# The element order of the gate copy: contiguous read and stepped write in place of stepped read and short-run write

## The chip, the cores and the metric

The kernel runs on one core of one Trainium2 chip. The time is device microseconds of that core for one execution. Five engines take part: TensorE (PE in the profile, its weight loads PEld), VectorE (DVE), ScalarE (ACT), GpSimd (POOL) and SyncE (SP), which here only issues DMA transfers.

## The reference

One layer of a streaming encoder for 512 tokens of width 1024: a token-mixing half (windowed attention beside a gated position mixer), and then a PEER channel mixer. The change lies in the channel mixer. It picks, for each token and each of 8 heads, 16 experts out of 16384 and sums them with softmax weights:

```
q = (xt @ w_query).reshape(T, PEER_HEADS, 2, D_HALF)
s = jnp.einsum('thpd,hpnd->thpn', q, sub_keys)
top_s, top_i = lax.top_k(s, PEER_TOPK)
...
ids = i1 * N_KEYS + i2                 # expert = key 1 * 128 + key 2
gates = softmax(best_s)
a = jnp.einsum('tkd,td->tk', expert_down[idb], xb)
act = gelu(a) * gb
y = jnp.einsum('tk,tkd->td', act, expert_up[idb])
```

## The kernel before, in words

The first stages (up to about 446 us of the trace) make the token-mixing half and the scores, and pick 128 experts for each token. Of the 512 tokens, 128 are done by gathering their experts' rows. For the other 384 all 16384 experts are multiplied densely, in 128 tiles of 128 experts; the tile's result is multiplied by a gate that is zero where the token did not pick the expert.

These dense gates are made in the **gate stage**, which is where the change lies. For each token, a 128 x 128 matrix (key 2 on the partitions, key 1 along the row) is the product of two small matrices that hold one row for each of the token's 128 picks: `onehot2` (a 1 at the pick's key 2) and `gated1` (the gate at the pick's key 1). The work goes in 48 turns of 8 tokens, with two sets of buffers used in turn (u = 0, 1). In each turn:

- DVE writes six of the eight onehot2 matrices in one instruction (line 1117) and six of the eight gated1 matrices in six instructions (line 1121).
- POOL writes the other two gated1 matrices (line 525), after it has copied their scalars (line 522).
- ACT writes the other two onehot2 matrices (lines 757 and 761).
- PE multiplies (line 1463): two groups (s = 0, 1) of four tokens, each group into one PSUM bank. The group s = 0 waits for DVE alone, the group s = 1 for POOL and ACT too. Before it overwrites a bank it waits for the copy of two turns ago.
- ACT copies each bank (128 partitions x 512 elements: four tokens t with 128 keys i each) into `stage` (line 766), an SBUF tile that holds 128 keys x 128 tokens in each partition, so that the tokens of one key lie side by side and one key is 512 bytes from the next.

ACT's program runs in this order: the two copies of turn m, then its part of the one-hot rows of turn m + 2. The stage tiles are two; every 16 turns (one block of 128 tokens) SyncE writes a full one to device memory (lines 406 and 426): the first two blocks while the gate stage runs, the third in four pieces after it. The tiles' gates are read back from there in the last stage.

The last stage (from 574 us to the end) is a loop over the 128 tiles of experts: down product (lines 1482 to 1484), Gelu (line 793), times the gate (line 1166), up product (lines 1493 to 1495). Its first down weights are in SBUF while the gate stage still runs; ACT rounds them (line 787) right after its last gate copy.

Of the kernel before, what the change touches and what calls it, by code (L numbers as in the profile page):

```python
# [66 lines left out]
TB = 8  # L67
# [58 lines left out]
def build_block(nc, x, c, w_ada, b_ada, g_pre_mix, g_post_mix, g_pre_ffn, g_post_ffn, w_in, attn_sinks,  # L126
                sgu_norm, sgu_w, sgu_b, w_out, peer_query, peer_keys, peer_down, peer_up, down_t, out):
    ctx = ExitStack()
    with ctx:
# [109 lines left out]
        stage = [r(f"stage{i}", [KEYS, P]) for i in range(2)]  # L239
# [29 lines left out]
        bank = [ctx.enter_context(nc.psum_tensor(f"bank{i}", [P, 512], F32)) for i in range(8)]  # L269
# [305 lines left out]
        def _(act):  # L575
# [187 lines left out]
            def gates_out(b, i, u):  # L763
                for s in range(2):
                    act.wait_ge(pe_g, b * 32 + 4 * i + 2 * u + s + 1)
                    act.activation(
                        stage[b % 2][:, :, bass.ds(i * (2 * TB) + u * TB + 4 * s, 4)],
                        bank[1 + 2 * u + s][:].rearrange("p (t i) -> p i t", t=4),
                        ACT.Copy).then_inc(act_g, 1)

            for u in range(2):
# [2 lines left out]
            for b in range(GB):  # L774
                if b >= 2:
                    act.wait_ge(stored[b % 2], 16)
                with act.Fori(0, turns - 1 if b == GB - 1 else turns) as i:
                    for u in range(2):
                        gates_out(b, i, u)
                        hot_rows(b * 2 * turns + 2 * i + u + 2, u)  # L780
            for u in range(2):
                gates_out(GB - 1, turns - 1, u)
# [749 lines left out]
```

## Time and profile before

| | |
|---|---|
| time, median of 3 runs | 1676.28 us (1675.06 to 1676.77) |
| profiled execution, its own time | 1676.28 us |
| its span | 1674.2 us |
| mean granted TensorE clock | 0.964 |
| PE busy | 1509.4 us (90%) |
| DVE busy | 1192.8 us (71%) |
| ACT busy | 632.3 us (38%) |
| POOL busy | 711.3 us (42%) |

Busy shares are means over stages that are limited by different engines, so the stage around the change has to be read by itself. The gate copies run from 453.65 to 573.97 us of the span. The granted clock is a share of the full 2.4 GHz.

### The profile page before, as it was taken

The page shows a single profiled execution, that of the slowest core. Times are in us where ns is not written, and L with a number is a line of the kernel's source. Part 1 is how long each engine was busy: PE and PEld are TensorE (multiplying, and loading weights), DVE is VectorE, ACT ScalarE, POOL GpSimd, SP SyncE. Part 2 cuts the span into 40 slices and gives each one's busy share as a digit, 9 for nine tenths or more (in the row PEclk, how much of TensorE's full clock was granted, in tenths as well). Part 3 has the DMA queues.
Part 4 walks back from the last instruction along what each step waited for, and adds up shares of the span by engine and source line. Part 5 has one row for each costly group of instructions (what it writes and reads, how often), then busy time and mean ns, then how long its engine had stood idle before and what let it go on. Part 6 is the DMA issues. An engine that isn't in the chain of part 4 may idle for free.

```text
span 1674.2 us, 25887 instructions
## 1 busy us (share of the span) xinstructions
PE 1509.4 (90%) x7686; PEld 1291.7 (77%) x7686; DVE 1192.8 (71%) x2424; ACT 632.3 (38%) x1018; POOL 711.3 (42%) x715
## 2 busy tenths in 40 slices
PE   4999989676288779999999999999999999999995
PEld 3475537554277769999999999999999999999994
DVE  6545437999799748777777777777777777777776
ACT  1114324333488623333333333333333333333332
POOL 0000003555599627544444444444444444444441
PEclk9999999887599989999999999999999999999998
DMA  9942201110017899877777777877777778777762
GB/s 325 372 176 101 76 25 38 50 50 13 0 53 212 250 344 362 302 274 276 273 275 275 281 273 277 277 279 276 278 276 276 278 276 277 279 276 276 278 242 100
DMA packets 186503, 372.34 MB, mean 222 GB/s; under 512 B 19753, under 2 KB 103281, under 8 KB 186481
## 3 DMA queue, kind: packets, MB, share of 16 engines
q1 hardware_dynamic: 149088, 237.57, 42.5%
q0 software_dynamic: 36864, 134.23, 22.0%
q10 hardware_dynamic: 528, 0.26, 0.1%
q8 instruction: 11, 0.18, 0.0%
q14 instruction: 12, 0.09, 0.0%
HBM read 344.76 MB, written 27.26 MB: 222 GB/s over the span
## 4 chain that ended last, share of the span: by engine, by line
PE 63%; DVE 12%; issue 4%; DVEq 2%; SPq 1%; DMA 1%; ACT 1%; POOL 0%; POOLq 0%; ACTq 0%
PE bank L1482 10%; PE bank L1484 10%; PE bank L1483 10%; PE bank L1494 10%; PE bank L1495 10%; PE bank L1493 10%; DVE gated L1121 4%; DVE topi L1030 1%; DVEq L1121 1%; SPq L406 1%; DVE top L1027 1%; DVE cand L1052 1%; DVE pick L1045 1%; DVE score L1034 1%; DVE onehot L1117 1%
## 5 line engine op out<-in xcount | busy, mean ns | idle before, releaser
L1482 PE MATMUL bank<-h2hi,dhi 128*128 128x384 f32 x1024 | 345.4, 337 | 14.6 <-DVE dlo L1135 14.6
L1484 PE MATMUL bank<-h2hi,dlo 128*128 128x384 f32 x1024 | 345.2, 337 | 0.0
L1483 PE MATMUL bank<-h2lo,dhi 128*128 128x384 f32 x1024 | 344.5, 336 | 0.0
L1495 PE MATMUL bank<-uhi,alo 128*128 128x512 f32 x768 | 301.3, 392 | 0.0
L1494 PE MATMUL bank<-ulo,ahi 128*128 128x512 f32 x768 | 301.0, 392 | 0.0
L1493 PE MATMUL bank<-uhi,ahi 128*128 128x512 f32 x768 | 298.6, 389 | 0.0
L543 POOL COPY idx_u<-ids 128x1 uint32 (+1 forms) x128 | 112.7, 881 | 343.6 <-DVE y L1156 343.5
L1166 DVE TENSOR_TENSOR acts<-gel,gate 128x384 f32<-128x384 f32 x128 | 71.5, 559 | 257.1 <-ACT gel L793 234.0
L545 POOL DMA_INDIRECT rows_u<-in_peer_up,idx_u x128 | 199.9, 1562 | 99.0 <-POOL idx_u L543 99.0
L1482 PEld LDWEIGHTS bank<-h2hi,dhi 128*128 128x128 f32 x1024 | 193.6, 189 | 20.4 <-DVE dlo L1135 10.1
L1483 PEld LDWEIGHTS bank<-h2lo,dhi 128*128 128x128 f32 x1024 | 193.4, 189 | 4.8
L1484 PEld LDWEIGHTS bank<-h2hi,dlo 128*128 128x128 f32 x1024 | 193.3, 189 | 0.0
L802 ACT ACTIVATE ahi<-acts 128x384 fp32r<-128x384 f32 x128 | 67.1, 524 | 329.1 <-PE bank L1495 321.6
L793 ACT ACTIVATE gel<-bank 128x384 f32<-128x384 f32 x128 | 62.9, 492 | 338.9 <-PE bank L1484 338.9
L1135 DVE TENSOR_TENSOR dlo<-down,dhi 128x1024 fp32r<-128x1024 f32 x128 | 156.7, 1225 | 45.4 <-ACT dhi L787 45.4
L545 POOL DMA_INDIRECT rows_d<-in_peer_down,idx_d x128 | 130.6, 1020 | 104.3 <-POOL idx_d L543 97.6
L1156 DVE SCALAR_TENSOR_TENSOR y<-rows_u,coef,y 128x1024 f32<-128x1024 f32 x128 | 164.0, 1281 | 5.2 <-DVE coef L1150 5.0
L1495 PEld LDWEIGHTS bank<-uhi,alo 128*128 128x128 f32 x768 | 144.1, 188 | 30.3
L1144 DVE SCALAR_TENSOR_TENSOR junk<-rows_d,h2nat 128x1024 f32<-128x1024 f32 x128 | 157.0, 1227 | 14.6 <-DVE y L1156 7.5
L1494 PEld LDWEIGHTS bank<-ulo,ahi 128*128 128x128 f32 x768 | 144.1, 188 | 27.7
L1493 PEld LDWEIGHTS bank<-uhi,ahi 128*128 128x128 f32 x768 | 144.3, 188 | 27.2
L1177 DVE TENSOR_TENSOR ulo<-up,uhi 128x1024 fp32r<-128x1024 f32 x128 | 156.6, 1224 | 0.9 <-ACT uhi L804 0.8
(202 smaller groups left out, 2224.1 us busy)
## 6 DMA issues: line engine op xcount, KB each, us to landing
down<-in_down_t SPq DMA_DIRECT2D x128, 512.0 KB, 4.4
up<-in_peer_up SPq DMA_DIRECT2D x128, 512.0 KB, 3.4
ada<-in_w_ada SPq DMA_DIRECT2D x12, 2048.0 KB, 16.2
gate<-gates_dram SPq DMA_DIRECT2D x128, 192.0 KB, 4.0
gates_dram<-stage SPq DMA_DIRECT2D x2, 8192.0 KB, 30.4
wq<-in_peer_query SPq DMA_DIRECT2D x16, 512.0 KB, 4.0
gates_dram<-stage SPq DMA_DIRECT2D x4, 2048.0 KB, 14.3
w_in_sb<-in_w_in SPq DMA_DIRECT2D x2, 2048.0 KB, 20.0
```

Of the source, the lines that this page charges most:

```text
L543: ch.link(gp.tensor_copy(idx[k][:], ids[:, bass.ds(n, 1)]))
L545: return gp.indirect_dma_start(rows_[k][:], None, table[0], bass.IndirectOffsetOnAxis(ap=idx[k][:, 0:1], axis=0))
L1135: ve.tensor_tensor(dlo[s][:], down[s][:], dhi[s][:].bitcast(F32), ALU.subtract).then_inc(dve_dlo, 1)
L1144: ve.scalar_tensor_tensor(out=junk[:], in0=rows_d[k][:], scalar=1.0, in1=h2nat[:], op0=ALU.mult, op1=ALU.mult, accum_out=dots[:, k:k + 1]) ...
L1156: ve.scalar_tensor_tensor(out=y[:], in0=rows_u[k][:], scalar=coef[:, k:k + 1], in1=y[:], op0=ALU.mult, op1=ALU.add).then_inc(dve_add, 1)
L1177: ve.tensor_tensor(ulo[s][:], up[s][:], uhi[s][:].bitcast(F32), ALU.subtract).then_inc(dve_ulo, 1)
L1482: pe.matmul(bank[s][:, 0:TD], dhi[s][:, k, :], h2hi[:, k, 0:TD], start=k == 0, stop=False)
L1483: pe.matmul(bank[s][:, 0:TD], dhi[s][:, k, :], h2lo[:, k, 0:TD], start=False, stop=False)
L1484: last = pe.matmul(bank[s][:, 0:TD], dlo[s][:, k, :], h2hi[:, k, 0:TD], start=False, stop=k == KT - 1)
L1493: pe.matmul(got[:], ahi[s][:, tokens], uhi[s][:, half], start=first, stop=False)
L1494: pe.matmul(got[:], ahi[s][:, tokens], ulo[s][:, half], start=False, stop=False)
L1495: done = pe.matmul(got[:], alo[s][:, tokens], uhi[s][:, half], start=False, stop=last)
```

## The change

One instruction of the gate stage, the copy from a PSUM bank to `stage`, goes over the same 512 elements of each partition in another order. Before, key is the outer and token the inner dimension; after, token is the outer and key the inner.

```
                     act.activation(
-                        stage[b % 2][:, :, bass.ds(i * (2 * TB) + u * TB + 4 * s, 4)],
-                        bank[1 + 2 * u + s][:].rearrange("p (t i) -> p i t", t=4),
+                        stage[b % 2][:, :, bass.ds(i * (2 * TB) + u * TB + 4 * s, 4)].rearrange("p i t -> p t i"),
+                        bank[1 + 2 * u + s][:].rearrange("p (t i) -> p t i", t=4),
                         ACT.Copy).then_inc(act_g, 1)
```

| | PSUM read | SBUF write |
|---|---|---|
| before | each element 128 words (512 bytes) from the one before, every fourth time back | runs of 4 adjacent words (16 bytes), then 512 bytes on |
| after | 512 adjacent words | each element 512 bytes from the one before, 128 times, then back and one word on |

The same values land at the same addresses. No instruction is added, removed or moved on any engine, and every wait and every signal stays; the copy occurs 96 times (48 turns x 2 banks).

## Rows read from the trace of the kernel before

**Rows 1.** The page, part 1: busy time of each engine over the span.
```profile
PE 1509.4 (90%) x7686; PEld 1291.7 (77%) x7686; DVE 1192.8 (71%) x2424; ACT 632.3 (38%) x1018; POOL 711.3 (42%) x715
```

**Rows 2.** Chain of work that ended last, 560 to 640 us: start, length, what.
```profile
564.92 1.00 DVE gated L1121 x4
566.93 1.50 DVE gated L1121 x6
...
571.29 2.06 PE bank L1463 x16
573.37 0.61 ACT stage L766
574.07 8.69 DMA gates_dram<-stage
```

**Rows 3.** Busy time in two stretches; PEclk is the granted clock.
```profile
core 0: us, PE busy (x) PEld busy (x) DVE busy (x) ACT busy (x) POOL busy (x), PEclk, DMA share, GB/s
480.00:520.00 40.00, 32.53 (x256) 29.56 (x256) 40.00 (x113) 34.86 (x81) 37.19 (x49) 1.00 0.65 184
520.00:560.00 40.00, 32.51 (x256) 29.55 (x256) 40.00 (x113) 34.87 (x80) 37.19 (x49) 1.00 0.74 208
```

**Rows 4.** Timeline of one turn: start, length, instruction, in brackets the idle before it.
```profile
565.92 0.60 ACT L766 ACTIVATE stage<-bank 128x512 f32 x1 [0.29 <-PE bank L1463]
566.26 2.05 PE L1463 MATMUL bank<-gated,onehot 128*128 128x128 f32 x16 [0.47 <-DVE gated L1121]
566.41 0.68 ACT L757 ACTIVATE onehot<-iota,pickT 128x128 f32<-128x128 f32 x2
566.92 1.72 DVE L1121 TENSOR_SCALAR gated<-iota,pickT 128x128 f32<-128x128 f32 x6
567.13 0.51 ACT L761 ACTIVATE onehot<-onehot,ones 128x256 f32<-128x256 f32 x1
567.55 0.60 ACT L766 ACTIVATE stage<-bank 128x512 f32 x1
568.44 0.60 ACT L766 ACTIVATE stage<-bank 128x512 f32 x1 [0.29 <-PE bank L1463]
568.57 0.94 DVE L1117 TENSOR_TENSOR onehot<-iota,pickT 128x768 f32<-128x768 f32 x1
```

**Rows 5.** Who waited for whom, 460 to 560 us: total, times, longest.
```profile
PE bank L1463 <- DVE gated L1121: 18.7, 40, 0.5
ACT stage L766 <- PE bank L1463: 11.8, 41, 0.3
```

**Rows 6.** Waits of the SP queue, 440 to 640 us.
```profile
SPq L410 <- DMA gates_dram<-stage: 30.0, 1, 30.0
SPq L426 <- ACT stage L766: 8.0, 1, 8.0
```

**Rows 7.** Groups of ACT instructions over the span: busy us, mean ns, idle before.
```profile
L679 ACT ACTIVATE wqhi<-wq 128x1024 fp32r<-128x1024 f32 x16 | 16.7, 1047 | 0.0
L793 ACT ACTIVATE gel<-bank 128x384 f32<-128x384 f32 x128 | 62.9, 492 | 338.9 <-PE bank L1484 338.9
L766 ACT ACTIVATE stage<-bank 128x512 f32 x92 | 54.8, 597 | 16.5 <-PE bank L1463 16.5
L718 ACT ACTIVATE score<-bank 128x512 f32<-128x512 f32 x16 | 8.9, 596 | 1.4 <-PE bank L1434 1.3
L624 ACT ACTIVATE kT<-bank 128x512 f32<-128x512 f32 x1 | 0.6, 597 | 7.2 <-PE bank L1328 7.2
```

**Rows 8.** Timeline of ACT at the start of the gate copies.
```profile
455.35 0.60 ACT L766 ACTIVATE stage<-bank 128x512 f32 x1 [1.11 <-PE bank L1463]
455.85 0.68 ACT L757 ACTIVATE onehot<-iota,pickT 128x128 f32<-128x128 f32 x2
456.56 0.51 ACT L761 ACTIVATE onehot<-onehot,ones 128x256 f32<-128x256 f32 x1
456.98 1.06 ACT L766 ACTIVATE stage<-bank 128x512 f32 x2
457.93 0.69 ACT L757 ACTIVATE onehot<-iota,pickT 128x128 f32<-128x128 f32 x2
```

**Rows 9.** A group of POOL instructions over the span.
```profile
L499 POOL TENSOR_TENSOR hit<-hit,topf 128x1024 f32<-128x1024 f32 x16 | 37.6, 2369 | 1.1 <-ACT hit L728 1.1
```

**Rows 10.** Timeline of PE, 380 to 386 us.
```profile
380.06 0.76 PE L1393 MATMUL bank<-h2hi,wqhi 128*128 128x512 f32 x1 [6.38 <-POOL wqlo L483]
...
382.33 0.63 PE L1395 MATMUL bank<-h2hi,wqlo 128*128 128x512 f32 x1
...
385.34 0.40 PE L1393 MATMUL bank<-h2hi,wqhi 128*128 128x512 f32 x1
```

**Rows 11.** Busy time and granted clock of two stretches there.
```profile
376.00:384.00 8.00, 3.94 (x10) 3.15 (x11) 7.97 (x52) 5.48 (x6) 8.00 (x4) 0.57 0.23 66
384.00:392.00 8.00, 8.00 (x44) 6.83 (x43) 7.90 (x36) 2.53 (x4) 3.06 (x2) 1.00 0.00 0
```

**Rows 12.** Timeline of ACT at the end of the gate copies.
```profile
572.48 0.60 ACT L766 ACTIVATE stage<-bank 128x512 f32<-128x512 f32 x1 [1.02 <-PE bank L1463]
573.37 0.60 ACT L766 ACTIVATE stage<-bank 128x512 f32<-128x512 f32 x1 [0.29 <-PE bank L1463]
573.87 1.99 ACT L787 ACTIVATE dhi<-down 128x1024 fp32r<-128x1024 f32 x2
```

## The prediction

> **What bounds the kernel now.** I start with the busy shares of the whole span: PE leads with 90%, ACT stands at 38% [rows 1]. That would say that nothing done to ACT matters. But a share over the span is a mean over stages, so I go to the stage that holds the copy. The chain of waits near its end reads, turn after turn, "DVE gated", and only at the very end PE, one copy of ACT, and then the store [rows 2]. The stretches of 40 us inside the stage say the same: DVE is busy for 40.00 of 40.00 us, ACT for 34.9, POOL for 37.2, PE for 32.5 at a granted clock of 1.00 [rows 3]. So DVE sets the pace of the gate stage, and ACT, at 87%, is not far behind. The whole question is how far.
>
> The timeline of one turn answers it [rows 4]. The second copies of two turns in a row start at 565.92 and 568.44, so a turn takes about 2.51 us (2.52 between rounded numbers; 48 turns are 120.5 us, and the copies run for 120.3 us). In each turn ACT waits for PE once, 0.29 us before the second copy (11.8 us in 41 waits between 460 and 560 us [rows 5]). That is less than ACT's true slack, because the first copy also starts before PE has finished the second bank. The true need of ACT is the time from start to start when it waits for nothing:
>
> - second copy to the first one-hot instruction: 566.41 - 565.92 = 0.49 us [rows 4];
> - the one-hot instructions up to the next copy: 567.55 - 566.41 = 1.14 us [rows 4];
> - the first copy when the second follows with no wait: 457.93 - 456.98 = 0.95 us for the two, less 0.49 for the second, is 0.46 us [rows 8].
>
> The sum is 2.09 us a turn against DVE's 2.51. The slack is 0.42 us a turn, 0.21 us for each of the two copies.
>
> **The change part by part.** It removes, adds and moves no instruction. It has two parts, both inside the copy.
>
> The read becomes contiguous. Today each element lies 512 bytes from the last, and the copy takes 597 ns. Copies of the same size that read PSUM in one run take 596 ns (scores) and 597 ns (keys) [rows 7]. So the stepped read costs nothing today, and the contiguous one gains nothing: 0. Even a faster copy would gain nothing, since ACT is not the bound of the stage; what a faster copy could save is its own 0.1 us once, at the end.
>
> The Trainium skill ("SBUF — State Buffer", Specifications) says that PSUM has 8-byte lines, SBUF 16-byte ones, and that an access which crosses to a new line every time pays. The 597 ns of the present copy, which hops lines on every read, does not bear this out for ACT's reads from PSUM. Its half on PSUM would give the contiguous read a gain, and the trace gives none; its half on SBUF would charge the new write, which puts one word in a line in place of four, but it has no figure.
>
> The write becomes stepped. Today it writes four adjacent words and then hops 512 bytes; after the change every word is a hop. No row of the trace has an ACT write of single words, so its price has to be bounded.
>
> - Lower end: a hop costs nothing, as it does on the read side and as the present hop after every fourth word does (597 ns against 596 [rows 7]). The copy stays at 0.60 us.
> - Upper end: nothing but a slower engine's pace is at hand. POOL takes 2369 ns for 1024 elements, 2.31 ns each [rows 9]. ACT's own element costs (597 - 492) / 128 = 0.82 ns, from its copies of 512 and 384 elements out of PSUM, with 597 - 512 x 0.82 = 177 ns fixed [rows 7]. At POOL's pace the copy would take 177 + 512 x 2.31 = 1360 ns, 0.76 us more.
> - The value that I take: each word needs one more step of ACT, so 512 elements cost what 1024 do. By the slope that is 597 + 512 x 0.82 = 1017 ns; the row of a 1024-element instruction reads 1047 ns [rows 7]. I take 1.03 us, 0.43 us more. It lies between the two ends and it is the nearest ACT row that takes more steps. I choose it above the lower end because the two hops are not alike: the free one in today's write comes once in four words, the new one comes with each word, so that there is nothing for it to hide behind.
>
> The Trainium skill has a measurement of the same kind, on another engine ("Vector Engine (DVE) Microarchitecture Reference", Measured stream behaviour on trn2): a VectorE op whose destination hops on every element takes 1.71 ns a column in place of 1.05, runs of two or more words are free, and one that steps by 24 words takes 2.50 ns. No run here shows it. With 1.71 ns the copy would be an estimated 177 + 512 x 1.71 = 1.05 us, and the end 22 us later.
>
> Now the sum. With 0.43 us more for each copy ACT needs 2.09 + 0.86 = 2.95 us a turn, more than DVE's 2.51, and it becomes the bound. Does anything else stop it at that pace? The order on ACT is copies of turn m, one-hot rows of turn m + 2. PE's group for turn m + 1 needs the one-hot rows that ACT finished before the copies of turn m, and PE needs 2.05 us for both groups [rows 4], less than 2.95. DVE may start turn m + 2 when PE is done with turn m, and it needs 2.51. So PE and DVE wait, and ACT does not.
>
> I place it in time from the rows. The second copy of turn 0 starts at 455.35 [rows 8], since it waits for PE and not for ACT. The copies of turn 1 then start at 455.35 + 0.49 + 0.43 + 1.14 = 457.41. Turns 1 to 45 have copies and one-hot rows: 45 x 2.95 = 132.75, so the copies of turn 46 start at 590.16. The last two turns have four copies and no one-hot rows: three at 0.46 + 0.43 and the last for its full 1.03, 3.70 us, and the end is at 593.86. Today it is at 573.37 + 0.60 = 573.97 [rows 12]. The gate stage becomes 19.9 us longer.
>
> **What hides it? Nothing.** After its last copy ACT goes on with rounding the down weights at 573.87 [rows 12], for which PE waits, and the store of the third block starts at 574.07, the next piece of the chain [rows 2]. SyncE had waited 30.0 us for the second block's store and then still 8.0 us for ACT's last copy [rows 6]. So neither the store nor the early loads are late; with a slower gate stage they are only earlier in comparison. From there all is as today, 19.9 us later. The profiled execution took 1676.28 us for a span of 1674.2, so 2.1 us lie around the span, and it is also the median of the runs. Forecast: 1676.3 + 19.9 = 1696 us, 1.2% slower. For copies between 1.01 and 1.07 us the same sum gives 1694 to 1700.
>
> **The rivals.**
>
> *A. The hop is free, or smaller than the slack: not slower.* ACT's writes leave at one word a step wherever they go, as its reads come in. The point from which it decides is 0.21 us a copy, that is 0.81 us: below that DVE keeps the pace of 2.51 us. For it: the read side and the present 16-byte runs at 597 ns. Against it: no row shows single-word writes. Time: 1676 us, at most 0.4 us more for the last two copies. Any gain would have to come out of a DVE that is never idle, and the copy does not touch it.
>
> *B. The hop costs more than a step.* Price by POOL's pace: a copy of 1.36 us, a turn of 2.09 + 1.52 = 3.61 us. The same placing gives 457.74 + 45 x 3.61 + 3 x 1.22 + 1.36 = 625.2, 51 us later: 1727 us. For it: the new step is the same power of two each time, so that successive words may meet in the same part of the memory. Against it: today's reads use the same step at full rate. The skill's 2.50 ns for a step of 24 words (same page and section) would be an estimated 1.46 us a copy and about 60 us.
>
> *C. PE loses its clock.* PE would work 2.05 of 2.95 us, 69% in place of 82%. In an earlier stage, after an idle time of 6.38 us, matmuls that take 0.40 us at the full level took 0.63 [rows 10], and the granted clock of that stretch was 0.57, against 1.00 in the next [rows 11]. If the gate stage fell to the lower level of 1.2 GHz, 2.05 us of PE would become about 4 and PE would be the bound: 1.5 x 47 = 70 us more, 1746 us. Against it: the idle times would be under 1 us each.
>
> **How the numbers follow.** Chances: forecast 0.75; A 0.12; B 0.09; C 0.02; and 0.02 for a gain that I cannot place, such as a better meeting of DVE and PE. What a measurement of this kernel can tell from no change is about 0.2%, 3.4 us. The forecast, B and C are slower by more, which is 0.86; A is the case of no change, 0.12, and the last case is faster, 0.02. The range has to hold 0.8: the forecast's own range is 1692 to 1704 (copies of 0.99 to 1.11 us by the same sum), and A is reached at 1676. I take 1675 to 1710, which leaves out B and C.
>
> **What the profile after would show.** The mean of the copy at line 766 near 1030 ns in place of 597, with every other ACT group as before. In the middle of the gate stage a turn of 2.95 us, ACT busy the whole time, DVE at 2.51 / 2.95, 85%, waiting for PE, and PE waiting for ACT's one-hot rows in its second group. The copies end near 594 us; from there the trace is today's, shifted. The granted clock stays at 1.00. If the copy reads 597 ns or anything up to 810, rival A holds and the turn stays at 2.51 us. If it reads well over 1.1 us, it is B; if the matmuls of line 1463 lengthen instead, C. My prediction is wrong in its mechanism if the copy lengthens by 0.43 us and the turn does not reach 2.9, since then ACT has slack that I did not see.

## The result, and the profile after

The changed kernel takes 1691.51 us (median of 4 runs, 1690.55 to 1692.72) against 1676.35 us (4 runs, 1675.06 to 1676.77) for the kernel before. The ratio is 1.0092, with a 95% interval of 1.0075 to 1.0109. It is 15.2 us slower. Forecast were 1696 us and 19.9 us more, with 1675 to 1710 as the range; the range of the forecast's own case, 1692 to 1704, was missed by half a microsecond.

The copy itself, among the groups of ACT instructions over the span (against [rows 7]):

```profile
L766 ACT ACTIVATE stage<-bank 128x512 f32 x92 | 89.3, 1072 | 3.1 <-PE bank L1463 3.1
L793 ACT ACTIVATE gel<-bank 128x384 f32<-128x384 f32 x128 | 62.9, 492 | 344.2 <-PE bank L1484 344.2
L757 ACT ACTIVATE onehot<-iota,pickT 128x128 f32<-128x128 f32 x96 | 31.5, 378 | 0.0
```

It went from 597 to 1072 ns, and its idle time before it from 16.5 to 3.1 us: ACT no longer waits for PE. The other ACT groups have the length they had, but for the first one-hot instruction (line 757), whose mean went from 391 to 378 ns. The two stretches in the middle of the stage (against [rows 3]):

```profile
480.00:520.00 40.00, 32.43 (x226) 27.10 (x224) 36.85 (x101) 39.54 (x72) 36.56 (x44) 1.00 0.51 144
520.00:560.00 40.00, 32.42 (x225) 27.23 (x226) 36.86 (x100) 39.55 (x71) 36.74 (x43) 1.00 0.60 171
```

DVE fell from 40.00 to 36.86 us, ACT rose from 34.87 to 39.55, and the granted clock stayed at 1.00. The stage has changed hands. In the same time PE did 225 matmuls in place of 256 and the turn is that much longer. PE's busy time hardly fell, since the 16 matmuls of a turn are counted as busy for about 2.4 us in place of 2.05; the count is the better reading. DMA traffic does not matter to the copy: its mean is 1075 ns from 460 to 490 us, where the DMA share is 0.00, and 1071 ns from 500 to 530 us, where it is 0.99. Who waited for whom, 460 to 560 us (against [rows 5]):

```profile
PE bank L1463 <- ACT onehot L761: 13.6, 31, 0.5
DVE onehot L1117 <- PE bank L1463: 6.7, 30, 0.2
PE bank L1463 <- DVE gated L1121: 2.1, 5, 0.5
```

The line "ACT stage waits for PE" is gone, PE waits for ACT's one-hot rows, and DVE, which had no wait in this stretch before, waits for PE. One turn in the timeline (against [rows 4]):

```profile
542.57 1.92 ACT L766 ACTIVATE stage<-bank 128x512 f32 x2
542.57 1.70 POOL L525 TENSOR_SCALAR gated<-iota,own 128x128 f32<-128x128 f32 x2 [0.17 <-POOL own L522]
542.90 2.38 PE L1463 MATMUL bank<-gated,onehot 128*128 128x128 f32 x16 [0.44 <-ACT onehot L761]
544.23 0.96 DVE L1117 TENSOR_TENSOR onehot<-iota,pickT 128x768 f32<-128x768 f32 x1 [0.23 <-PE bank L1463]
544.28 0.65 ACT L757 ACTIVATE onehot<-iota,pickT 128x128 f32<-128x128 f32 x2
544.97 0.51 ACT L761 ACTIVATE onehot<-onehot,ones 128x256 f32<-128x256 f32 x1
545.38 1.93 ACT L766 ACTIVATE stage<-bank 128x512 f32 x2
```

ACT has no gap, and no wait hides under the overlapping copies: PE ended its last matmuls at 545.28, before the two copies start at 545.38. The two copies take 544.28 - 542.57 = 1.71 us from start to start, the one-hot rows 1.10, the turn 2.81. Over the whole stage it is 2.83 us, from the starts of turn 1 and of turn 46, the last four copies:

```profile
457.51 1.94 ACT L766 ACTIVATE stage<-bank 128x512 f32 x2
...
585.03 3.59 ACT L766 ACTIVATE stage<-bank 128x512 f32<-128x512 f32 x4
588.43 1.99 ACT L787 ACTIVATE dhi<-down 128x1024 fp32r<-128x1024 f32 x2
```

(585.03 - 457.51) / 45 = 2.834 us. The last copy ends at 588.62 in place of 573.97, 14.65 us later, and the same store follows it in the chain of waits (against [rows 2]):

```profile
583.04 1.08 ACT stage L766
584.12 0.47 ACT onehot L757 x2
585.03 3.60 ACT stage L766 x4
588.72 8.69 DMA gates_dram<-stage
```

Behind the store the chain has the same links, down to the transfer of down weights for which ACT and then PE wait, first before and then after the change:

```profile
607.21 5.51 DMA down<-in_down_t
```

```profile
621.87 6.30 DMA down<-in_down_t
```

It ends at 612.72 before and at 628.17 after, 15.45 us later. So the gate stage gives 14.65 us and these transfers 0.8. The two profiled executions lie 1692.26 - 1676.28 = 16.0 us apart, the medians 15.2; what is left is no more than single executions differ by.

### The profile page after: what moved, and what is told of

The parts are those of the page before. It is cut to its first block, busy times and chain, and to the rows that moved or that the text cites. A ratio compares the mean times of both kernels' runs of the same rounds, so it can differ in the third digit from the quotient of the medians.

```text
span 1690.5 us, 25887 instructions
## 1 busy us (share of the span) xinstructions
PE 1524.0 (90%) x7686; PEld 1298.7 (77%) x7686; DVE 1196.7 (71%) x2424; ACT 661.7 (39%) x1018; POOL 721.4 (43%) x715
## 4 chain that ended last, share of the span: by engine, by line
PE 65%; DVE 8%; issue 4%; ACT 4%; SPq 1%; DMA 1%; POOL 0%; ACTq 0%; DVEq 0%; POOLq 0%
PE bank L1482 10%; PE bank L1484 10%; PE bank L1483 10%; PE bank L1494 10%; PE bank L1495 10%; PE bank L1493 10%; PE bank L1463 3%; ACT stage L766 2%; DVE topi L1030 1%; SPq L406 1%; DVE top L1027 1%; DVE cand L1052 1%; DVE pick L1045 1%; DVE score L1034 1%; ACT onehot L757 1%
```

## The experiments

A step is ACT's time for one element of a row, 0.82 ns in the prediction. Theory S: a word written by ACT that is not next to the word written before it takes two steps of ACT; the order of the read does not matter; and what the copy adds counts from the point where ACT needs more than DVE. Rivals: the read order or the shape of the loop costs (R), each new run costs whatever its length (L), only full 16-byte runs are fast (Q), the distance of the hop matters (B, N), or the turn is set by handovers and not by ACT. Each ratio is to the kernel before, run on the same chip. A line with + shows what the run's kernel has; `...` and `<...>` stand for parts left out.

**Write in one run** (e1)

```
-  stage[b % 2][:, :, bass.ds(i * 16 + u * 8 + 4 * s, 4)].rearrange("p i t -> p t i")
+  stage[b % 2][:].rearrange("p i t -> p (i t)")[:, bass.ds(i * 2048 + u * 1024 + s * 512, 512)]
```

> The copy reads its PSUM bank in one run, as in the changed kernel, and writes it to 512 adjacent words of stage (the gates land in other places, so the output is not the reference's). Theory S, a written word that is not next to the word before it takes two steps of ACT and the read order costs nothing: the copy is back at 597 ns, the turn at 2.51 us, the time at 1676 us. Rival R, the cost lies in reading the bank in token-outer order or in anything else of the new loop but the write: the copy stays near 1072 ns and the time near 1691 us.

Measured: 1675.54 us, ratio 0.9994 (0.9984 to 1.0004), copies of 598 ns, in the groups of ACT between 460 and 560 us, as for the next ones:

```profile
L766 ACT ACTIVATE stage<-bank 128x512 f32 x80 | 47.8, 598 | 11.6 <-PE bank L1463 11.6
```

All of the loss is gone with the read left contiguous. It was the write.

**Hop on both sides** (e4)

```
+  stage[b % 2][:].rearrange("p i t -> p (i t)")[:, <the same 512 words>].rearrange("p (t i) -> p i t", t=4)
+  bank[1 + 2 * u + s][:].rearrange("p (t i) -> p i t", t=4)
```

> The copy both reads and writes with a step of 128 words on every element (key outer, token inner on both sides; the gates land in other places, so the output is not the reference's). Theory S: the write hop costs as in the changed kernel and the read hop adds nothing: 1072 ns, 1691 us. Rival: the two costs add, or the read hop was hidden only because the write had runs: over 1300 ns, over 1710 us. Rival R: with the old read order the copy is back at 597 ns, 1676 us.

Measured: 1692.32 us, ratio 1.0092 (1.0075 to 1.0109), copies of 1085 ns:

```profile
L766 ACT ACTIVATE stage<-bank 128x512 f32 x71 | 69.7, 1085 | 0.0
```

The read hop adds 13 ns to 1072 even when the write hops too. With e1 this settles R: the read order costs next to nothing in either company.

**Runs of two words** (e3)

```
+  stage[...].rearrange("p i (h t) -> p h i t", h=2)
+  bank[1 + 2 * u + s][:].rearrange("p (h t i) -> p h i t", h=2, t=2)
```

> The copy writes runs of two adjacent words (8 bytes) and then hops 512 bytes; it reads two keys' tokens in step. Theory S in its form by pairs: two adjacent words are enough, 597 ns and 1676 us. Rival L, each new run costs something whatever its length: today's 128 runs are hidden but 256 would cost half of what 512 do, about 830 ns, a turn of 2.56 us, 1678 us. Rival Q, only a full run of four words goes at full rate: 1072 ns and 1691 us.

Measured: 1675.77 us, ratio 0.9995 (0.9986 to 1.0005), copies of 619 ns:

```profile
L766 ACT ACTIVATE stage<-bank 128x512 f32 x80 | 49.5, 619 | 10.6 <-PE bank L1463 10.6
```

Twice as many hops as before cost 22 ns, where L said about 230. L and Q fall. Two adjacent words are enough, where they begin on an even word, as they do here.

**A short step** (e5)

```
+  stage[b % 2][:].rearrange("p i t -> p (i t)")[:, <the same 512 words>].rearrange("p (i t) -> p t i", t=4)
```

> As the changed kernel (token outer, key inner, contiguous read), but the 128 words of a token are written 4 words (16 bytes) apart in place of 128 words, into a window of 512 adjacent words (the gates land in other places, so the output is not the reference's). Theory S, a word not next to the last costs one more step whatever the distance: 1072 ns, a turn of 2.83 us, 1691 us. Rival B in its remaining form, small steps cost more than large ones: 1.5 us a copy or more, a turn over 3.6 us, over 1725 us. Rival N, only far hops cost: 597 ns, 1676 us.

Measured: 1695.30 us, ratio 1.0116 (1.0101 to 1.0130), copies of 1124 ns (the mean between 460 and 560 us), and, in the timeline of ACT, a turn of 544.61 - 541.69 = 2.92 us:

```profile
541.69 2.04 ACT L766 ACTIVATE stage<-bank 128x512 f32 x2
...
544.61 2.02 ACT L766 ACTIVATE stage<-bank 128x512 f32 x2
```

A step of 16 bytes costs what one of 512 does, and about 50 ns more. N falls. Rival B's price was not seen at either step; other steps were not tried, and the 50 ns have no cause here.

**One of the two copies** (e2): the new order for s = 1, the old one for s = 0.

> Only the second of the two copies of each turn (s = 1) has the new order, the first has the old one. Slack theory: ACT needs 2.09 us plus about 0.38 us = 2.47 us a turn, under DVE's 2.51, so the slow copies are fully hidden but for the last, 0.4 us: 1676 to 1677 us. Rival, no hidden slack and each longer copy delays the handover to PE: half of the loss, 1684 us.

Measured: 1676.85 us, ratio 1.0001 (0.9991 to 1.0011), copies of 835 ns in the mean of slow and fast ones. ACT is nearly full and yet nothing is lost, as the busy time of a stretch shows (columns as in [rows 3]):

```profile
480.00:520.00 40.00, 32.54 (x256) 29.76 (x256) 40.00 (x112) 39.48 (x81) 37.19 (x49) 1.00 0.64 183
```

The slack of 0.42 us a turn is real and takes one slow copy whole. This is the plainest sign that the change costs what is left over after the slack, and not what it adds. A busy share of 98.7% of ACT here goes with no loss, since DVE has 40.00 of 40.00.

**One ACT matrix less** (e7, on the changed kernel; DVE makes that matrix)

```
-BY_POOL, BY_ACT = 2, 2
+BY_POOL, BY_ACT = 2, 1
```

> The changed kernel with one of ACT's two one-hot matrices given to DVE (ACT makes one, DVE seven). Theory, ACT is the bound of the gate stage after the change and needs 2.83 us a turn: ACT falls to 2.83 - 0.35 - 0.11 = 2.37 us, DVE rises to 2.51 + 0.13 = 2.64 us, so the turn is 2.64 us and the time 48 x 0.19 = 9 us under the changed kernel, 1682 to 1683 us. Rival, the turn after the change is set by a handover between ACT, PE and DVE: no gain, 1691 us or more.

Measured: 1682.81 us, ratio 1.0040 (1.0026 to 1.0055), 8.7 us under the changed kernel; the same stretch:

```profile
480.00:520.00 40.00, 30.97 (x242) 28.18 (x243) 40.00 (x106) 38.04 (x61) 37.37 (x47) 1.00 0.59 163
```

With ACT relieved DVE is the bound again, at 100% and a longer turn of its own: in the timeline its first instructions of two turns start 2.65 us apart. So ACT's own work was the bound of the changed kernel: a turn set by handovers alone would have gained nothing.

```profile
540.67 1.08 DVE L1117 TENSOR_TENSOR onehot<-iota,pickT 128x896 f32<-128x896 f32 x1
...
543.32 1.08 DVE L1117 TENSOR_TENSOR onehot<-iota,pickT 128x896 f32<-128x896 f32 x1
```

**The slack spent the other way** (e8): the old copy, and `BY_ACT = (2, 3)` for u = 0, 1.

> The kernel before, with its old copy, where ACT makes three of the eight one-hot matrices in every second turn (two in the others) and DVE so many fewer. If DVE is the bound of the gate stage before and ACT has 0.42 us of slack a turn: DVE falls from 2.51 to 2.45 us a turn on average, ACT rises from 2.09 to 2.32, so the stage is 48 x 0.065 = 3 us shorter: 1673 us. Rival, the two turns don't even out (ACT needs 2.55 us in its long turn, more than DVE's 2.38 there): no change, 1676 us.

Measured: 1675.11 us, ratio 1.0001 (0.9990 to 1.0013). No gain can be told from the times. (The ratio goes by means, and one of the 12 runs took 1685.42 us; the median is 0.6 us under that of the kernel before.) The trace shows a small one: the copies run from 452.8 to 571.5 us, 118.7 us in place of 120.3. In the profile two turns take DVE 546.42 - 541.46 = 4.96 us, 2.48 each in place of 2.51, half of the gain that was expected. The smaller one-hot instruction gave what it should: from its start to the next instruction it is 542.20 - 541.46 = 0.74 us, against 544.77 - 543.90 = 0.87 for the larger. But the six instructions of gates behind it took 543.90 - 542.20 = 1.70 us up to the next turn, those of the other turn 546.42 - 544.77 = 1.65. These 0.05 us in two turns, two fifths of the 0.13 gained on the one-hot instruction, were not followed up.

```profile
541.46 0.81 DVE L1118 TENSOR_TENSOR onehot<-iota,pickT 128x640 f32<-128x640 f32 x1
542.20 1.73 DVE L1122 TENSOR_SCALAR gated<-iota,pickT 128x128 f32<-128x128 f32 x6
543.90 0.96 DVE L1118 TENSOR_TENSOR onehot<-iota,pickT 128x768 f32<-128x768 f32 x1
544.77 1.73 DVE L1122 TENSOR_SCALAR gated<-iota,pickT 128x128 f32<-128x128 f32 x6
546.42 0.81 DVE L1118 TENSOR_TENSOR onehot<-iota,pickT 128x640 f32<-128x640 f32 x1
```

**Runs that begin on an odd word** (e9 with runs of two, e10 with the old runs of four)

```
-  stage = [r(f"stage{i}", [KEYS, P]) for i in range(2)]
+  wide = r("stage0", [KEYS * P + 1])
+  stage = [wide[:, 1:KEYS * P + 1].rearrange("p (i t) -> p i t", t=P), r("stage1", [KEYS, P])[:]]
```

> As the kernel with runs of two words (618 ns a copy), but the first stage tile, which takes the first and the third of the three blocks of 16 turns, lies one word (4 bytes) further on, so that each run of two starts on an odd word; the second block is written as before. Theory G, what counts is the aligned pair of 8 bytes, and a word that is alone in its pair takes two steps: about 1072 ns in the first and third block and 618 in the second, 32 turns of 2.83 in place of 2.51 us, 1686 us. Theory A, adjacency is enough wherever the run starts: 618 ns in all blocks, 1676 us.

> The kernel before, with the first stage tile one word further on, so that its runs of four words lie as one, two and one in the aligned pairs; the second block is as before. Theory G: two of four words are alone and take a step more, 256 steps x 0.83 = 213 ns, about 810 ns a copy in the first and third block and 597 in the second; ACT needs 2.09 + 0.43 = 2.52 us a turn, so nothing shows: 1676 us. Theory A: 597 ns in all blocks, 1676 us.

Measured (groups of ACT instructions), e9 in the first block (460 to 490 us) and then in the second (500 to 530 us):

```profile
L767 ACT ACTIVATE stage<-bank 128x512 f32 x24 | 19.4, 840 | 0.0
...
L767 ACT ACTIVATE stage<-bank 128x512 f32 x24 | 14.9, 621 | 3.2 <-PE bank L1464 3.2
```

and e10 in the same two stretches:

```profile
L767 ACT ACTIVATE stage<-bank 128x512 f32 x24 | 17.7, 736 | 0.8
...
L767 ACT ACTIVATE stage<-bank 128x512 f32 x24 | 14.3, 597 | 3.5 <-PE bank L1464 3.5
```

Where the run begins does matter, so adjacency alone (theory A of these two runs) falls; but an odd start costs less than theory G said, 840 ns where it had 1072 and 736 where it had 810. The extra is 219 ns for 256 odd runs of two and 139 ns for 128 odd runs of four, 0.86 and 1.09 ns a run: about one step (0.82 ns) for each odd run, not one for each word that is alone in its pair of 8 bytes.

One account comes near all the copies, though no run was made to test it: what counts is the aligned group of 16 bytes (tiles begin at multiples of 32), and a word alone in its group takes about a step more. Of e9's odd runs half begin on the second word of such a group and lie in it whole, and half begin on the fourth and are split, which makes 256 lone words, 210 ns by the step; in e10 each run of four leaves one word alone, 128 in all, 105 ns. The changed kernel and e5 have 512 lone words, and 475 and 527 ns more than the kernel before, 0.93 and 1.03 ns each; e3 has none. A run whose pairs all begin on the second word, or all on the fourth, would decide; it was not made.

The time of e9 also says something of the slack. With copies of 840 ns in the first block DVE was busy all the time and a turn took 473.40 - 470.87 = 2.53 us, not the 2.83 that was expected from longer copies:

```profile
460.00:490.00 30.00, 24.37 (x193) 22.14 (x192) 30.00 (x85) 29.61 (x61) 27.89 (x37) 1.00 0.00 0
```

Both times were missed by more than the gate stage explains: e9 took 1683.43 us, ratio 1.0048 (1.0031 to 1.0065), e10 1684.23 us, ratio 1.0049 (1.0032 to 1.0066), though their last copies end at 573.0 and 573.7 us, no later than before. The loss lies in the last stage, as the next runs show. The odd tile had pushed six kinds of tiles of that stage (the down and up weights with their high and low parts, two buffers each) on by 32 bytes.

**Those tiles moved, and nothing else** (e12; e11 with the stage tiles moved too; e13 by 64 bytes)

```
-        r = Region(nc, stage_1_at, limit)
+        r = Region(nc, stage_1_at + 32, limit)
```

> The kernel before, unchanged but for the place of six tiles of the last stage (down, up and their high and low parts), which lie 32 bytes further on; the two kernels with an odd stage tile had moved them too and lost 7 to 8 us, none of it in the gate stage. Theory, the last stage is slower by the new place of these tiles (0.06 us for each of 128 tiles): 1683 to 1684 us. Rival, the loss came from reading and storing a stage tile that begins on an odd word: 1676 us.

> The kernel before with both stage tiles and the same six tiles 32 bytes further on, no odd words. Theory by place of the six tiles: 1683 to 1684 us with the copies at 597 ns. Rival by odd words: 1676 us.

> The kernel before with the six last-stage tiles 64 bytes further on in place of 32. If only the place modulo 64 bytes counts, it is back at the time of the kernel before, 1676 us. If the place within a larger frame counts, or any move away from the first place costs, it stays at 1683 to 1684 us; a third place could also be faster than the first, under 1673 us.

Measured: e12 1683.68 us, ratio 1.0045 (1.0028 to 1.0062); e11 1684.28 us, ratio 1.0049 (1.0032 to 1.0066); e13 1674.39 us, ratio 0.9999 (0.9989 to 1.0010). So 32 bytes cost about 8 us with no other change, and 64 bytes cost nothing. Busy time in the same stretch of 200 us, first of the kernel before, then of e12:

```profile
900.00:1100.00 200.00, 200.00 (x1013) 182.15 (x1012) 142.93 (x175) 71.19 (x104) 92.07 (x97) 1.00 0.79 277
```

```profile
900.00:1100.00 200.00, 200.00 (x1006) 180.66 (x1005) 141.47 (x174) 70.53 (x102) 92.56 (x96) 1.00 0.78 274
```

PE does 1013 matmuls in the first and 1006 in the second, at the same granted clock; e9 does 1007 and e10 1006 there. The rival, that the odd stage tile was slower to read or store, falls.

## Why the prediction was right

**The bound and the slack.** ACT's need of 2.09 us a turn and DVE's 2.51 gave a slack of 0.21 us a copy. e2 tested it directly: one copy of the two slow, nothing lost. e7 tested the bound: ACT relieved, the turn back at DVE's own 2.65 us.

**The read gains nothing.** So it was: e1 reads contiguously at 598 ns, and e4's stepped read adds 13 ns.

**The write costs a step for each word.** The chosen value was 1.03 us; measured were 1.07. The reason that was given, that a single word has no neighbour for the hop to hide behind, agrees with e3, two words at 619 ns. It is not the whole: in e9 each word has a neighbour too, and the copy takes 840 ns. The Trainium skill ("Vector Engine (DVE) Microarchitecture Reference", Measured stream behaviour on trn2) gives for VectorE 1.71 ns a column where the destination hops on every element, no cost for aligned runs of two, and 1.30 ns where both sources are read in pairs that begin on an odd word. The runs here have similar figures for ACT's write, with the prediction's 177 ns of fixed time taken off: (1072 - 177) / 512 = 1.75 ns for single words, (619 - 177) / 512 = 0.86 for pairs, and (840 - 177) / 512 = 1.29 for odd pairs, which here are written and not read. Its 2.50 ns for a step of 24 words has no counterpart in the two steps that were run.

**The term that was mis-sized.** The sum had 2.95 us a turn; it is 2.83. Over 45 turns this is 5.2 us, all of the difference between the forecast end of the copies, 593.86, and the real one, 588.62. The copy got longer by 475 ns as an instruction but only by (1.73 - 0.95) / 2 = 0.39 us from start to start, since slow copies overlap more: 1072 - 865 = 207 ns, where the old ones overlapped by 597 - 475 = 122. The sum had added the growth in length, 0.43, to the old distances. What ACT spends is the distance from start to start. The one-hot rows took 1.10 to 1.11 us in place of 1.14; their first instruction was the shorter one, and why is not shown.

The nearness of the forecast is in part luck. The copy was longer than the 1.03 us of the sum, and with 1.07 the same sum gives 1700 us, 8.5 too many; the length that was set too low hid part of the overlap that was left out.

By its own last sign the prediction's mechanism would be wrong: the copy lengthened by more than 0.43 us and the turn did not reach 2.9. The sign is right in that ACT had room that the sum did not see. But this room was no wait, as ACT had no gap; it was the overlap of successive copies. That ACT becomes the bound, with PE and DVE waiting for it, held. DVE was busy for 92% and not 85%, with a shorter turn and gates instructions whose end no longer overlaps the next turn's start (1.73 us of them, which the next instruction followed after 1.65 before).

**Nothing hides it.** The store follows the last copy as before, 14.65 us later, and the first transfer of down weights behind it ends 15.45 us later.

**The rivals.** A (free hop) fell with the first row of the profile after. Its threshold of 0.81 us a copy was too low as a length: in e2 and in the first block of e9 the mean copy took 835 and 840 ns and DVE still kept the pace. From start to start such a copy is shorter than that: with an overlap between the 122 and the 207 ns above, 0.63 to 0.72 us as an estimate, against the 0.475 + 0.21 = 0.69 us that the slack allows. B and C did not come: the copy was at 1.07 us and the clock at 1.00 from 480 to 560 us (0.99 over all the copies, before and after).

## What to carry to other kernels

When an access order can be chosen, give the runs of two adjacent words or more, beginning on an even word, to the SBUF write and the hops to the PSUM read; in these float32 copies on ACT the hop was free on the one side and cost a step a word on the other. Before pricing such an edit, work out what each engine of the stage needs a turn, from start to start where it waits for nothing: what an edit costs is what it adds beyond the difference to the bound. And add what an instruction's distance grows by, which was 0.39 us where its length grew by 0.475. And compare placements before blaming an edit for half a per cent: a tile that grows moves those behind it.

## What had not been expected of the hardware

Moving the weight tiles of the last stage by 32 bytes lengthened a tile's turn there from 8.31 to 8.37 us (23 turns between 1103.35 and 1294.41 us before, between 1106.13 and 1298.56 us in e12), 0.06 us a turn and 7.6 us over the 128 tiles, while 64 bytes changed nothing that can be told. Between 700 and 1600 us the first up product (line 1493) went from 389 to 394 ns a matmul, the other two from 392 to 394 and 395, and the down products from 335 or 336 to 336 or 337. Which of the tiles matters, and through which access, is open. And an odd start of a run costs ACT's write about one step a run, at runs of two and of four, where the pair of 8 bytes would have had it cost two; whether the group of 16 bytes is the reason is open.
